# Expert weights of an encoder block: the second expert's loads of a pair issued by ScalarE, the first's by the sync engine

## The reference

```
g_idx = argmax(xf @ w_rg + b_rg)                 # 1 of 4 groups for each token
top_vals, top_idx = top_k(e_logits of that group, 2)   # 2 of its 8 experts
e_gate = softmax(top_vals) * g_gate
hdn = silu(xb @ w_gate[e]) * (xb @ w_up[e])      # w_gate, w_up: 1024 x 512
out = hdn @ w_down[e]                            # w_down: 512 x 1024
y[token] += e_gate * out                         # then residual add
```

## Time and profile before

| | |
|---|---|
| time, median of 3 runs | 1752.48 us (1751.34 to 1753.69) |
| profiled execution, its own time | 1752.03 us |
| its span | 1750.0 us |
| PE busy | 1694.3 us (97%) |
| DVE, ACT, POOL busy | 712.6, 683.8, 668.4 us |
| q1, SP's transfers | 526.89 MB, 73.5% of the 16 engines' span |
| expert stage, layer 1 | about 420 to 876 us |
| expert stage, layer 2 | about 1288 to 1743 us |

### The profile page before, as it was taken

How to read it: one execution, slowest core, us unless ns; L and a number is a source line. 1 busy time by engine, 2 the same in 40 slices (tenths; PEclk the granted TensorE clock), 3 DMA queues, 4 the chain that set the end, 5 groups by cost and what they waited for, 6 DMA issues and landing times.

```text
span 1750.0 us, 23255 instructions
## 1 busy us (share of the span) xinstructions
PE 1694.3 (97%) x8996; PEld 1059.0 (61%) x8996; DVE 712.6 (41%) x1341; ACT 683.8 (39%) x1541; POOL 668.4 (38%) x536
## 2 busy tenths in 40 slices
PE   8999999999999999898999999999999999998997
PEld 5889877787434444343378898777864444443343
DVE  5728788524222212121266387865241212222122
ACT  5565787754211111111156567877541111111111
POOL 6888776895000000000077987768930000000000
PEclk9999999999999999999999999999999999999999
DMA  6544312766999999999954452227569999999997
GB/s 253 210 181 156 145 49 104 292 278 241 374 420 428 428 427 427 428 427 427 414 221 160 179 193 97 97 97 316 219 258 415 427 428 426 428 428 427 428 425 299
DMA packets 47523, 528.47 MB, mean 302 GB/s; under 512 B 5128, under 2 KB 7944, under 8 KB 17200
## 3 DMA queue, kind: packets, MB, share of 16 engines
q1 hardware_dynamic: 47376, 526.89, 73.5%
q0 software_dynamic: 32, 0.02, 0.0%
HBM read 525.82 MB, written 1.06 MB: 301 GB/s over the span
## 4 chain that ended last, share of the span: by engine, by line
PE 66%; DMA 11%; DVE 9%; SPq 5%; ACT 5%; issue 3%; POOL 1%; DVEq 0%; ACTq 0%
PE PS L1250 18%; DMA view<-in_w_exp_down_dram 10%; PE PS L1279 9%; PE PS L834 8%; PE PS L836 8%; PE PS L835 8%; SPq L658 5%; DVE view L1932 5%; PE PS L1197 2%; PE PS L1183 1%; DVE view L1928 1%; PE PS L1041 1%; ACT view L1503 1%; PE PS L1184 1%; PE PS L822 1%
## 5 line engine op out<-in xcount | busy, mean ns | idle before, releaser
L2299 POOL TENSOR_TENSOR view<-view,view 128x512 fp32r<-128x512 f32 x448 | 580.2, 1318 | 552.7 <-DVE view L1834 466.7
L1250 PE MATMUL PS<-view,view 128*64 128x512 f32 x2048 | 454.5, 596 | 21.7 <-issue 21.0
L1391 ACT ACTIVATE view<-view 128x512 fp32r<-128x512 f32 x448 | 274.9, 632 | 151.7 <-PE PS L836 147.3
L1250 PEld LDWEIGHTS PS<-view,view 128*64 128x64 f32 x2048 | 152.3, 137 | 295.5 <-issue 291.7
L834 PE MATMUL PS<-view,view 128*128 128x512 f32 x704 | 285.2, 405 | 5.7 <-POOL view L2299 3.3
L836 PE MATMUL PS<-view,view 128*128 128x512 f32 x704 | 275.0, 391 | 0.0
L835 PE MATMUL PS<-view,view 128*128 128x512 f32 x704 | 274.8, 390 | 0.0
L1279 PE MATMUL PS<-view,stb 128*64 128x512 f32 x1024 | 230.4, 597 | 8.7 <-DMA view<-in_w_exp_down_dram 5.9
L2199 DVE SCALAR_TENSOR_TENSOR view<-PS,gcol,view 128x512 fp32r<-128x512 f32 x64 | 48.1, 751 | 446.0 <-ACT view L1701 445.8
L834 PEld LDWEIGHTS PS<-view,view 128*128 128x128 f32 x704 | 132.3, 188 | 33.4 <-issue 5.7
L1279 PEld LDWEIGHTS PS<-view,stb 128*64 128x64 f32 x1024 | 71.7, 136 | 132.4 <-issue 115.2
(11 more groups left out here) (254 smaller groups left out, 2027.0 us busy)
## 6 DMA issues: line engine op xcount, KB each, us to landing
view<-in_w_exp_up_dram SPq DMA_DIRECT2D x60, 2048.0 KB, 26.5
view<-in_w_mix_dram SPq DMA_DIRECT2D x56, 2048.0 KB, 7.6
view<-in_w_exp_gate_dram SPq DMA_DIRECT2D x56, 2048.0 KB, 28.6
view<-in_w_exp_down_dram SPq DMA_DIRECT2D x56, 2048.0 KB, 29.8
view<-in_w_exp_down_dram SPq DMA_DIRECT2D x32, 512.0 KB, 11.4
view<-in_w_exp_gate_dram SPq DMA_DIRECT2D x8, 1024.0 KB, 10.4
view<-in_w_exp_gate_dram SPq DMA_DIRECT2D x16, 512.0 KB, 32.5
view<-in_w_exp_up_dram SPq DMA_DIRECT2D x16, 512.0 KB, 15.4
```

The lines of the kernel that those rows point to most:

```text
L1250: ins = pe.matmul(bank(ph, name, j)[e * CAP:(e + 1) * CAP, :], xgT1[:, k, at + e * CAP:at + (e + 1) * CAP], slot8[expert_block(j, kind, e) ...
L1391: nc.scalar.activation(highs(chunk), weights(slot8, chunk), ACT.Copy).then_inc(*high_ready.up(ph))
L2299: g_.tensor_tensor(weights(low8, chunk), weights(slot8, chunk), highs(chunk), ALU.subtract).then_inc(*low_ready.up(ph))
```

## The change

From block 21 on (n above 2*SLOTS = 20) and before the last pair (n below 90), the odd blocks, which are those of the second expert of a pair, are no longer in SP's list. ACT issues them, on its own DMA queue, from `load_second`, which is called at three places in ACT's program of pair j: after the silu for block 6*j + 11 (down of pair j + 1), after the high rows of the pair before for block 6*j + 9 (up of pair j + 1), and after the copy of the hidden rows for block 6*j + 13 (gate of pair j + 2). The slots, the conditions on which a block may be loaded, the signals and PE's waits are the same. The line `check_made` that goes counts signals while the program is built and is no instruction.

```diff
--- before.py
+++ after.py
@@ -568,6 +568,10 @@
             n, slot = expert_block(j, kind, e)
             return loaded[slot].at(ph, ring_loads[slot] + sum(parts_of(m) for m in range(n % SLOTS, n + 1, SLOTS)))
 
+        def from_act(n):
+
+            return n % 2 == 1 and 2 * SLOTS < n < 6 * ALL_PAIRS - 6
+
         def all_passed(eng, of, ph):
 
             for b in range(8):
@@ -723,6 +727,8 @@
                     for n in (SLOTS + 2, SLOTS + 3):
                         load_part(n, part, 2)
                 for n in range(SLOTS + 4, 6 * ALL_PAIRS - 6):
+                    if from_act(n):
+                        continue
                     sp.wait_ge(*used(n - SLOTS))
                     load(n // 6, n % 6 // 2, n % 2)
                     if n == 2 * SLOTS:
@@ -740,7 +746,6 @@
                     for part in range(QUARTERS):
                         for n in (first, first + 1):
                             load_part(n, part, QUARTERS, tail_loaded[kind][part])
-                check_made(ph, {f"loaded{s}": loaded[s] for s in range(SLOTS)})
                 with sp.If(over > 0):
                     all_passed(sp, filled, ph)
                     with sp.Fori(1, PASSES) as b:
@@ -1637,13 +1642,25 @@
                 nc.scalar.activation(r1[:, 5, :], r1[:, 4, :], ACT.Exp).then_inc(*rexp.up(ph))
                 check_made(ph, {"high_ready": high_ready, "tile_high": tile_high, "sumsq": sumsq, "u_ready": u_ready,
                                 "softa": softa, "p_ready": p_ready, "rexp": rexp, "L_ready": L_ready})
+                def load_second(n, used):
+
+                    if from_act(n):
+                        j, kind, slot = n // 6, n % 6 // 2, ORDER[n % SLOTS]
+                        src = (w_exp_gate, w_exp_up, w_exp_down)[kind][ds(l * EXPERTS + 2 * j + 1, 1)]
+                        act.wait_ge(*used)
+                        act.dma_start((slot4 if kind == 2 else slot8)[slot].rearrange("p k f -> p (k f)"),
+                                      src.rearrange("a p f -> p (a f)")).then_inc(*loaded[slot].up(ph))
+
                 for j in range(ALL_PAIRS):
                     gate(ph, j)
+                    load_second(6 * j + 1 + SLOTS, full(ph, "g", j))
                     if j:
                         high_rows(ph, j - 1, 1)
+                        load_second(6 * j - 1 + SLOTS, full(ph, "y2", j - 1, 1))
                     if j == 0:
                         selection_out(ph, j)
                     hidden_out(ph, j)
+                    load_second(6 * j + 3 + SLOTS, full(ph, "u", j))
                     if j:
                         selection_out(ph, j)
                     if gathered(j):
```

## The result

The changed kernel takes **1782.16 us** (median of 4 runs, 1780.69 to 1784.74) against 1752.22 us (4 runs, 1751.34 to 1753.69): ratio 1.0167, 95% interval 1.0155 to 1.0179. It is slower by 30 us. 1772 was predicted, with a range of 1757 to 1788. The profiled execution took 1784.74 us, with a span of 1782.7.

What follows compares the result with a forecast made beforehand. At each layer's end, transfers up to pair 14 bind, then PE's own work with almost no slack. Order costs of 8.5 and 8.6 us plus 3 us of lag make 20 us over 1752: 1772 us, range 1757 to 1788.

Steps and rivals of the forecast that it cites:

- The price of the order: End of each layer: second up blocks land behind second down blocks, delaying pairs 13 and 14; +8.5 and +8.6 us.
- Half share: DMA engines in the expert stages: each queue gets half, so a block takes 9.8 us in its queue.
- rival of an uneven share: Expert stages: ACT's queue gets under half, +18 us a layer, 1790 us; chance 0.11 together with a lower rate.
- Rate with two queues: Expert stages: between +1.9% and -2.8%, -4 to +6 us a layer; taken as 0, at 427 GB/s.
- rival "faster": Expert stages: two queues keep engines fuller, 427 to 435 GB/s, 15 us gained at best, 1737 us; chance 0.10.
- Nothing in steady state: Middle of the stages: engines stay busy, a pair still takes 29.4 us, so the new order costs nothing there.
- ACT's issue at no cost: ACT's program: three issues a pair of 0.4 us each fit idle time; cost 0, at most 5 us a layer.
- SP's stall, no gain: SP's queue at the tail: the 11.14 us stall at one issue shrinks, but the gain is counted at nothing.
- The lag between the queues: ACT's queue may run behind SP's, bounds 0 and some 4 us a layer; 1.5 us taken, 3 us in all.
- the pairing of the landings: A pair's landings: both gates together, then first up with second down, then first down with second up.
- gaps of "some 5 us each": PE in 720 to 840 us: gaps before the up matmuls of odd pairs, hardly any before gate or down matmuls.

Runs made afterwards that it cites:

- e2: Against the kernel before: one queue, all loads on SP, each second up block from block 21 on issued behind its pair's second down block; 1771.62 us, ratio 1.0107.
- e6: Against the change: block 21 stays in SP's list and ACT begins with block 23; 1773.68 us, ratio 1.0116.
- e5: The change run a second time, with no edit, as a base on the chip of the next runs; 1781.47 us, ratio 1.0162.
- e7: Against the change: ACT loads only odd blocks 21 to 47, SP all the others; 1753.34 us, ratio 1.0003.
- e4: Against the change: 14 small matmuls on PE ahead of the up-block wait of pairs 5, 7, 9, 11 and 13; 1778.28 us, ratio 1.0145.
- e3: Against the change: ACT issues the second up block after the next pair's silu, ahead of the down block; 1761.24 us, ratio 1.0047.
- e8: Against the change: ACT issues in order of need and in time, its first load waiting until block 19 has landed; 1761.31 us, ratio 1.0042.

## Why the prediction was right in sign and 10 us short

The three runs e2, e6 and e5 make a ladder against their own runs of before: the order in one queue is +18.3 us; moving it onto two queues with block 21 on SP makes it +21.1 (1773.68 less 1752.63), 2.8 more; taking block 21 too adds 7.8. That is the change's 28.8 in that set of runs (1781.47 less 1752.63).

- **The price of the order: right.** Predicted were 8.5 and 8.6 us, 17.1 in all; e2 measured 18.3. The 1.2 us between them fits the slow matmuls that it also has (8.78 for 7.09 us, 1.7 us in layer 1), which the sum did not hold. The up matmuls of pair 13 moved by 9.6 us in e2 against 9.7.
- **Half share: right.** A block every 9.7 to 9.9 us on each queue. The rival of an uneven share falls, though its time (1790) was nearer to the result than the forecast (1772), which is luck and speaks for no uneven share.
- **Rate with two queues, taken unchanged: right.** 426 to 428 GB/s in every window. The rival "faster" needed 435. The Trainium skill, page DMA: Bandwidth & Descriptors, section Issuing engines are not separate DMA queues, says that DMAs issued by several engines run on the same 16 DMA engines. The unchanged 427 GB/s agree with it. It says nothing on order, and most of the 30 us lie there.
- **Nothing in steady state: right**, as e7 shows. PE waits 4.67 us at one place in the middle of e7, and its time is before's. The slow matmuls in the middle of the change, 8.7 of the 10.4 us, fall under the same rule, which is why e4, which took them away with the one at the end, won 3 to 5 us and not 20.
- **ACT's issue at no cost: right.** ACT's timeline in pair 12 has the issues beside the activations:

```profile
788.62 0.60 ACT L1688 ACTIVATE view<-PS 128x512 f32<-128x512 f32 x1 [10.92 <-PE PS L1255]
788.63 0.35 ACTq L1651 DMA_DIRECT2D view<-in_w_exp_down_dram  x1
789.82 0.69 ACT L1718 ACTIVATE view<-PS,gcol 128x512 fp32r<-128x512 f32 x1 [0.59 <-PE PS L1189]
```

  The high rows follow the silu by the same 0.59 us of idle time as in the earlier trace rows. Not even the gap was used: the 0.35 us of issue lie inside the silu's 0.60.
- **SP's stall, no gain: right as far as shown.** No run changes it by itself. In SP's timeline the eight quarters of the tail that took 25.78 us to issue take 11.78 now, at the same DMA share:

```profile
826.95 11.78 SPq L662 DMA_DIRECT2D view<-in_w_exp_gate_dram  x8
```

- **The lag between the queues: this is the step that failed, and the pairing of the landings with it.** The prediction had the second up block land with the first down block, and gave ACT's queue a lag of 1.5 us a layer, "below the middle" of bounds of 0 and 4 us, because the second up block goes out 8 to 9 us late. That pairing is what e6 has. In the change the second up block lands beside the next pair's first gate block, one block later (1700.4 and 1700.2 us). e3 shows that the late issue gives next to nothing, and e6 that block 21 at the start of the split gives most of it. Counted from the start of the stage, pair 13's up matmuls start 1.2 and 1.0 us later than in e2 when block 21 stays on SP (e6, layers 1 and 2). They start 5.1 and 4.5 us later in e5, and 6.7 and 5.6 us in the first run of the change, outside my bounds. In time, e2 to e6 is 2.8 us for both layers and e6 to e5 7.8 us, 10.6 in all where I had 3, and some 3 us of these 10.6 are slow matmuls (the next point). I had bounded the lag by the delay of one issue, where a whole block on the wrong side of the start was possible. Pair 13's up matmuls start 16.2 us behind before's in the first run of the change (818.08 less 801.52 and 0.32), where 9.7 and the 1.5 of the lag were forecast.
- **The clock: a term that was missing.** It is worth 3 to 5 us (e4), of which part lies in e2's 18.3 already. The sum put it at nothing without a word, and the trace of before shows it: in layer 2 one wait has slow matmuls behind it (PE's timeline, first row below), and the granted clock of the window that holds them is 0.74 (second row). Layer 1 of before has waits of the same length without it (2.55 us at 733.02, then 7.09 us).

```profile
1599.46 8.63 PE L1250 MATMUL PS<-view,view 128*64 128x512 f32 x32 [2.55 <-issue]
...
1600.00:1605.00 5.00, 5.00 (x20) 1.69 (x18) 0.00 (x0) 0.00 (x0) 0.00 (x0) 0.74 0.99 423
```

  The forecast of gaps of "some 5 us each" before odd pairs came nearly true (3.1 to 4.9 us in layer 1, up to 5.4 in layer 2), and I should have asked what PE's speed is after them.
- **A misread row, without effect.** Of the earlier trace rows the prediction says 420 to 428 GB/s for slices 12 to 20 and 33 to 40. Slice 20 has 414 and slice 40 has 299: the plateaus are slices 12 to 19 and 32 to 39.

In layer 2 it went the same way. Its up matmuls of pair 13 waited 4.73 us and then ran long:

```profile
1700.48 9.81 PE L1255 MATMUL PS<-view,view 128*64 128x512 f32 x32 [4.73 <-issue]
...
1765.68 7.09 PE L1284 MATMUL PS<-view,stb 128*64 128x512 f32 x32
```

The last down matmuls end at 1772.8 against 1740.1, 32.7 us later, about 16 of them from layer 1.

None of the kernels beat the one before. The nearest, e7, equals it.

## What to carry to other kernels

Where one queue is full and serves blocks in the order in which they are needed, look at its order before you split it. Here a second queue added no bandwidth (427 GB/s with one and with two), it left each queue with half the rate, and a block issued behind one that is needed later landed a step of 9.8 us late. When a stream is split all the same, keep the order of need within each queue and count the blocks that each holds at the moment of the split, since here a queue that started one block heavier stayed so to the end of the stage. Read the cost at the end of the stage, where no transfer is left to wait for, and not from the sum of waits: in the middle the same waits cost nothing (e7). And read both layers of a trace: in the kernel before, slow matmuls behind a wait stand in layer 2 alone, and in the change only layer 2 shows plainly which blocks land together.

## What the runs showed of the hardware that was not expected

**PE's clock after a wait.** The windows of the changed kernel around pair 13's wait:

```profile
814.00:818.00 4.00, 0.10 (x1) 0.00 (x0) 1.95 (x3) 0.69 (x1) 0.00 (x0) 1.00 1.01 430
818.00:822.00 4.00, 3.92 (x12) 1.49 (x14) 0.00 (x0) 0.00 (x0) 0.00 (x0) 0.57 1.01 426
822.00:827.00 5.00, 5.00 (x25) 1.88 (x22) 0.09 (x1) 0.00 (x0) 0.00 (x0) 1.00 0.99 419
```

PE idles for 3.98 us, and in the four us after it the granted clock is 0.57, which is the lower level of 1.2 GHz most of the time; then it is 2.4 GHz again. PE's 32 matmuls take 8.79 us for 7.09. In the 14 us before this wait PE was busy all the time, at a granted clock of 1.00. After 4.67, 4.93 and 4.73 us of waiting the matmuls took 8.48, 9.50 and 9.81. After waits of 0.97, 1.58 and 1.90 us (e4) they took 7.09. In between it went both ways: 2.41 us (e4, layer 2) and 2.55 us (before, layer 2) were followed by 8.78 and 8.63 us, while 2.55 us (before, layer 1), 2.63 us (the change, layer 2) and even 3.51 us (e3, layer 2) were followed by 7.09. So the length of the wait alone does not decide it, and what does is open.

**Engines out of step.** With two full queues the 16 DMA engines finish the same block up to 12.2 us (the change) and 15.5 us (e8) apart in layer 1, with one queue at most 4.4 us, at the same 427 GB/s. It is not two queues alone that do it: in layer 2 of the change it is 4.6 us at most, and in e4, with the same two queues, 3.9 and 4.3. What sets it is open. It hides a late block from the averages, since the DMA share and the GB/s do not change.
